# A hybrid decoder step on one core: pooling released from the convolution loop, layer norm's sums inside projection blocks, first output blocks in halves

## The reference

```
h = rmsnorm(x); p = h @ w_in            # columns: conv value | conv gate | pool input, 1024 each
a = v * sigmoid(gate)                   # GLU
y = causal depthwise conv(a), 31 taps   # 8 tiles of 128 channels
yc = silu(layernorm(y + b_dw))          # mean and variance over the 1024 channels
s  = trailing mean of u over 2/4/8/16 positions - u   # 4 groups of 256 channels
yp = (s @ w_pool[group]) * pool_scale
x = x + concat(yc, yp) @ w_out
x = x + hierarchical_moe(rmsnorm(x))    # one group of 4, two of its 8 experts, SwiGLU
return rmsnorm(x), and the last inputs of conv and pooling as new states
```

## Time and profile before

| | us |
|---|---|
| median of 3 executions | 1366.17 |
| lowest and highest | 1365.81, 1368.48 |
| the profiled execution | 1363.6 |
| its span in the trace | 1361.7 |
| TensorE busy in the span | 1257.5 (92%) |
| VectorE, ScalarE, GpSimd busy | 345.9, 115.1, 111.0 |

### The profile page before, as it was taken

The page is one execution under the profiler, slowest core; times in us unless marked ns, Lnnn a source line. Parts: engine busy times, 40 slices in busy tenths (PEclk is TensorE's granted clock), DMA queues, the critical chain, the costliest instruction groups (busy, mean ns, idle before and its releaser), DMA issues.

```text
span 1361.7 us, 16051 instructions
## 1 busy us (share of the span) xinstructions
PE 1257.5 (92%) x6424; PEld 706.8 (52%) x6424; DVE 345.9 (25%) x692; ACT 115.1 (8%) x253; POOL 111.0 (8%) x167
## 2 busy tenths in 40 slices
PE   9999998999999999998989898898989898998894
PEld 7777776777765444454443444444434354444331
DVE  5599963110242110111101011110101011020216
ACT  2100014000210000000000000000000000000003
POOL 3211164000000000000000000000000000000000
PEclk9999999999999999999999999999999999999997
DMA  8544325665459999999999999999999999999985
GB/s 246 167 154 151 124 93 169 215 247 185 152 208 411 424 425 429 427 429 426 429 425 428 427 426 428 425 423 425 424 427 425 429 424 426 417 420 415 388 353 196
DMA packets 82886, 465.13 MB, mean 342 GB/s; under 512 B 7999, under 2 KB 50111, under 8 KB 56691
## 3 DMA queue, kind: packets, MB, share of 16 engines
q1 hardware_dynamic: 77184, 456.41, 82.1%
q0 software_dynamic: 5392, 7.87, 1.9%
q10 hardware_dynamic: 283, 0.48, 0.1%
HBM read 457.20 MB, written 20.80 MB: 351 GB/s over the span
## 4 chain that ended last, share of the span: by engine, by line
DMA 46%; PE 36%; issue 7%; DVE 5%; POOL 3%; SPq 1%; ACT 1%; DVEq 0%; POOLq 0%
DMA arena<-in_w_up_dram 43%; PE bank L759 19%; PE bank L589 11%; DVE arena L1061 3%; PE bank L737 2%; DMA stage<-in_w_down_dram 2%; PE bank L780 2%; POOL arena L1456 1%; DMA arena<-expert_rows 1%; SPq L415 1%; PE bank L674 1%; DMA arena<-in_g_final_dram 1%; POOL arena L1465 0%; PE bank L671 0%; POOL arena L1462 0%
## 5 line engine op out<-in xcount | busy, mean ns | idle before, releaser
L759 PE MATMUL bank<-arena,stage 128*64 128x512 f32 x1920 | 439.4, 611 | 57.0 <-DMA arena<-in_w_up_dram 56.9
L759 PEld LDWEIGHTS bank<-arena,stage 128*64 128x64 f32 x1920 | 145.8, 141 | 343.9 <-issue 304.4
L589 PE MATMUL bank<-arena,stage 128*128 128x288 f32 x1280 | 315.8, 408 | 2.9 <-ACT arena L921 1.5
L589 PEld LDWEIGHTS bank<-arena,stage 128*128 128x128 f32 x1280 | 241.5, 190 | 69.7 <-ACT arena L921 2.0
L737 PEld LDWEIGHTS bank<-x1w,x1r 128*128 128x128 f32 x1536 | 173.9, 192 | 25.2 <-issue 25.2
L737 PE MATMUL bank<-x1w,x1r 128*128 128x128 f32 x1536 | 179.9, 277 | 0.0
L1311 DVE TENSOR_TENSOR a_sb<-sl_sb,bank 128x256 f32<-128x256 f32 x32 | 19.5, 609 | 492.8 <-ACT sl_sb L963 492.8
L780 PE MATMUL bank<-arena,aT 128*64 128x512 f32 x512 | 113.4, 595 | 8.5 <-ACT aT L965 8.5
L1061 DVE SCALAR_TENSOR_TENSOR arena<-arena,wdw 128x256 f32<-128x256 f32 x240 | 102.9, 505 | 0.0
L1473 POOL DMA_INDIRECT expert_rows<-ysb,cur_d x31 | 30.3, 978 | 854.2 <-DVE ysb L1331 827.6
L1331 DVE TENSOR_SCALAR ysb<-bank,wslot 128x512 f32<-128x512 f32 x31 | 23.3, 751 | 254.7 <-PE bank L780 254.7
(11 more groups left out here) (262 smaller groups left out, 483.5 us busy)
## 6 DMA issues: line engine op xcount, KB each, us to landing
arena<-in_w_gate_dram SPq DMA_DIRECT2D x48, 2048.0 KB, 13.9
arena<-in_w_up_dram SPq DMA_DIRECT2D x48, 2048.0 KB, 20.7
arena<-in_w_down_dram SPq DMA_DIRECT2D x30, 2048.0 KB, 17.7
xT<-in_w_down_dram SPq DMA_DIRECT2D x15, 2048.0 KB, 19.8
stage<-in_w_down_dram SPq DMA_DIRECT2D x15, 2048.0 KB, 21.6
arena<-in_w_gate_dram SPq DMA_DIRECT2D x16, 1536.0 KB, 14.8
arena<-in_w_up_dram SPq DMA_DIRECT2D x16, 1536.0 KB, 21.1
stage<-in_w_in_dram SPq DMA_DIRECT2D x11, 2048.0 KB, 8.4
```

Of the source, the lines that this page charges most:

```text
L589: last = pe.matmul(ps[bank][:, 0:NTOK], wsl[a][:, k, cc * P:(cc + 1) * P], rhs[:, k, :], start=(n == 0), stop=(n == KT - 1))
L759: mm = pe.matmul(ps[4 + s][BLK * h:BLK * (h + 1), :], xgT[:, k, BLK * s:BLK * (s + 1)], w[:, :, 256 * h:256 * (h + 1)], start=(k == 0), st ...
```

## The change

There are four edits. The products for new tokens (`prod`) move from `arena` to the tile `ysb`, which is unused until later, GpSimd's loop over the passes is unrolled, and its wait for the end of a pass stands at the head of passes 1 to 3 alone: nothing makes the pooling wait for the fourth pass any more. TensorE's mean product moves into the middle of the sixth pooling-input block, and its variance product ahead of the eighth. The first two w_out blocks are cut in halves, conv channels first, and two of these halves stand between and behind the last w_pool products. ScalarE's list is reordered to suit.

```diff
-        prod = words(arena, O_ST, 2 * NS * W).rearrange("p (c t w) -> p c t w", c=2, t=NS)
+        prod = ysb[:, :, :].rearrange("p s f -> p (s f)")[:, 0:2 * NS * W].rearrange("p (c t w) -> p c t w", c=2, t=NS)
...
-                    dense(2 * c + cc, c, cc, hT).then_inc(u_mm, 1)
-            pool_inputs(0)
-            pool_inputs(1)
-            pool_inputs(2)
-            pe.wait_ge(sum_ready, 1)
-            channel_sum(4, sqw[:, 4:6, :]).then_inc(sum_mm, 1)
-            pool_inputs(3)
-            pe.wait_ge(sq_ready, 1)
-            channel_sum(5, sqw[:, 0:2, :]).then_inc(sumsq_mm, 1)
+                    if m == 3 and cc == 1:
+                        pe.wait_ge(sq_ready, 1)
+                        channel_sum(5, sqw[:, 0:2, :]).then_inc(sumsq_mm, 1)
+                    dense(2 * c + cc, c, cc, hT, between=sum_of_channels if m == 2 and cc == 1 else None).then_inc(u_mm, 1)
+            def sum_of_channels():
+                pe.wait_ge(sum_ready, 1)
+                channel_sum(4, sqw[:, 4:6, :]).then_inc(sum_mm, 1)
+            for m in range(4):
+                pool_inputs(m)
...
+            def out_half(cc, h):
+                for k in range(CT * h, CT * h + CT):
+                    if h == 0 and cc == 0:
+                        pe.wait_ge(mix_ready, k + 1)
+                    last = pe.matmul(ps[cc][:, 0:NTOK], wsl[1][:, k, cc * P:(cc + 1) * P], mixT[:, k, :],
+                                     start=(k == 0), stop=(k == KT - 1))
+                return last
+            for i in range(6):
+                pooled(i)
+            pe.wait_ge(slot_in[1], 16 * 7)
+            out_half(0, 0)
+            pooled(6)
+            pooled(7)
+            out_half(1, 0)
             pe.wait_ge(wp_ready, CT)
-            pooled_first = tuple(range(CT, KT)) + tuple(range(CT))
+            for cc in range(2):
+                out_half(cc, 1).then_inc(o_mm, 1)
...
-            for n in range(6):
+            for n in range(5):
                 pool_line(n)
             act.wait_ge(sum_mm, 1)
             act.activation(nmean[:, :], ps[4][:, 0:NTOK], ACT.Copy, scale=-1.0 / DC).then_inc(nmean_ready, 1)
             act.wait_ge(centred, 1)
             act.activation(words(arena, O_AW, CT * NTOK), words(arena, O_YC, CT * NTOK), ACT.Square).then_inc(squared, 1)
+            pool_line(5)
+            act.activation(preload[:, :], ones[:, 0:1], ACT.Sqrt)
             pool_line(6)
-            pool_line(7)
             act.wait_ge(var_ready, 1)
             act.activation(lnr[:, :], lnv[:, :], ACT.Sqrt).then_inc(sqrt_done, 1)
+            act.activation(silu_table[:, :], ones[:, 0:1], ACT.Silu)
+            pool_line(7)
+            act.wait_ge(yn_ready, 1)
+            for j in range(4):
+                swish(j)
             for i in range(CT):
...
+                pooled(i)
+                if i < 4:
+                    swish(4 + i)
...
-            with pool.Fori(0, 4) as g:
-                ch.loop(g, 1)
+            for g in range(4):
+                if g:
+                    pool.wait_ge(conv_chain, PERC * g)
...
-                pool.wait_ge(conv_chain, PERC * (g + 1))
-            ch.end(4)
+            pool.wait_ge(work_ready, 4)
```

More of the change, by code:

```diff
@@ L652, in _, with pooled @@
             pe.wait_ge(var_ready, 1)
-            for i in range(CT):
+            def pooled(i):
                 g, dd = NG - 1 - i // 2, i % 2
@@ L681, in projection @@
                         pe.wait_ge(slot_in[a], 16 * o + (16 * 7 if a else 16 * 8))
-                    if first and q == 0:
-                        dense(q % 2, a, q % 2, mixT, order=pooled_first, late=(mix_ready, CT)).then_inc(o_mm, 1)
+                    if first and q < 2:
+                        pass
                     elif last and q == 3:
@@ L902, in pool_line, with pooled, swish @@
                          ps[c][:, SEQ:NTOK].rearrange("p (s t) -> p s t", s=NSEQ)).then_inc(u_evac[c // 2], 1)
-            for n in range(6):
+            def pooled(i):
+                act.wait_ge(wp_mm, i + 1)
+                j = CT - 2 - 2 * (i // 2) + i % 2
+                act.activation(mixT[:, CT + j, :], ps[4 + i % 2][:, 0:NTOK], ACT.Copy, scale=pps[:, j:j + 1]).then_inc(wp_ready, 1)
+            def swish(j):
+                act.activation(mixT[:, j, :], yc[:, j, :], ACT.Silu, bias=plb[:, j:j + 1], scale=plg[:, j:j + 1]).then_inc(mix_ready, 1)
+            for n in range(5):
                 pool_line(n)
@@ L909, in _ @@
             act.activation(words(arena, O_AW, CT * NTOK), words(arena, O_YC, CT * NTOK), ACT.Square).then_inc(squared, 1)
+            pool_line(5)
+            act.activation(preload[:, :], ones[:, 0:1], ACT.Sqrt)
             pool_line(6)
-            pool_line(7)
             act.wait_ge(var_ready, 1)
             act.activation(lnr[:, :], lnv[:, :], ACT.Sqrt).then_inc(sqrt_done, 1)
-            for i in range(CT):
[L915 to L921, removed]
+            act.activation(silu_table[:, :], ones[:, 0:1], ACT.Silu)
[3 more added lines that the diff above has]
+                swish(j)
+            for i in range(CT):
+                pooled(i)
+                if i < 4:
+                    swish(4 + i)
             for n, (b, r) in enumerate(((6, AK), (7, AK), (2, UK), (3, UK))):
```

## The result

The changed kernel took 1360.37 us (median of 5, 1358.76 to 1362.09), the kernel before 1368.02 (median of 5, 1365.81 to 1369.84); the ratio is 0.9943, with a 95% interval from 0.9926 to 0.9960, so 5.5 to 10.1 us faster. Forecast was 1371.3, 0.4% slower. Run again later beside other kernels the changed one was at 0.9963 (0.9948 to 0.9977), 3.1 to 7.1 us faster. The two intervals share 5.5 to 7.1 us. The rival "the pass is not held up", with a chance of 0.15, had said 1359.7, a gain of 6.5 us.

What follows compares the result with a forecast made beforehand. The expert-weight stream, started by TensorE, was taken as the bound, carrying mixer changes to the end. Profiled 1363.6 + 9.9 stall + 1.7 low clock - 6.5 tail = 1368.7; with 2.6 for the median, 1371.3 us, range 1362 to 1376.

Steps and rivals of the forecast that it cites:

- the pass is not held up: Fourth convolution pass: GpSimd waits or passes VectorE's taps, no stall, tail's gain alone, 1359.7 us; chance 0.15.
- The bound and the transfer: Mixer to expert weights: the weight stream starts with TensorE, so each mixer microsecond reaches the end one for one.
- the sum: Whole kernel: 1363.6 + 9.9 + 1.7 - 6.5 = 1368.7, plus 2.6 from profiled execution to median, 1371.3 us.
- The tail's gain: Transposes to third w_out block: 27.3 us instead of 33.8, a gain of 6.5 us.
- The new load wait: First half w_out block: its chunk lands 8.1 us after T, wanted at T + 7.7, so 0.4 us wait.
- the halves hide the last group's wait: Mixer tail: the seventh w_pool product comes at T + 11.5, so the 2.71 us wait for pooling goes.
- What the released pooling costs: Fourth convolution pass: 17 pooling instructions take turns with VectorE's taps, and the pass loses 12.9 us.
- The price: Fourth pass: a GpSimd instruction of length p costs the taps p - 0.25, together 12.9 us.
- GpSimd got its second product in against a queue of ready taps: Fourth pass: the argument given against the rival in which the pass is not held up, chance 0.15.
- the stall of 9.9: TensorE in the sixth pooling-input block: waits from 186.4 until `sum_ready` at 196.3, 9.9 us.
- the low clock of 1.7: TensorE's first products behind the stall run at the low clock, costing 1.7 us, 0 to 3 as ends.
- a loss of 9.6 us: Fourth pass: lower end of the forecast's own case, losses 9.6 to 17.1, 1367.5 to 1376 us, chance 0.65.

Runs made afterwards that it cites:

- the twins: Changed kernel with each fourth-pass tap waiting for its immediate predecessor: pooling beside the pass 1377.96 us, pooling held behind it 1372.91 us.
- The memset: Changed kernel with four small GpSimd instructions (a 128-column memset, two copies, an addition) ahead of the pooling: 1358.91 us in one execution.
- the kernels with three gaps: Changed kernel with the fourth pass written out and three of its taps (first of the pair at 14, 18, 22) waiting for their immediate predecessor: 1372.73 us, 1.0045.
- with none: Changed kernel with the fourth convolution pass written out behind a loop of three and no gap in it: 1360.78 us, 0.9937.

## Why the prediction was wrong

- **The bound and the transfer** held as far as the first expert product: it starts 141.6 us behind the third block in both traces. Behind it "one for one to the end" is shown only within the scatter of the weight streaming, 978 to 983 us, and the twins' medians don't show it. The base had moved as well, from 1366.17 (3 executions) to 1368.02 (5), which the sum could not know.
- **The tail's gain** held: 6.5 us predicted, 6.4 in the trace. The new load wait was 0.2 at most, ScalarE's 0.43 instead of 0.1. That the halves hide the last group's wait was a wrong reason: the release and the early order did it before them.
- **"What the released pooling costs"** is the step that failed. It took from L1441 that a GpSimd instruction waiting beside ready taps gets the port after one of them, and so a loss of 12.9 us. Measured loss beside the taps: none, 25.73 us for the pass as before; the addition waited 17 us instead, and TensorE did not stall. The price was not wrong for a case where turns are taken (12.1, 12.9 and 13.0 us measured for 12.9), but the case was. The products at 152.69 and the copy at 154.82 were issued within 0.1 us of GpSimd's last turn; the pooling's first addition comes 5.8 us behind it. "GpSimd got its second product in against a queue of ready taps" is not in the rows either: the product was issued at 152.69, 0.12 us ahead of the first two-input tap at 152.81, and it was the tap that waited. Nothing in the trace of before showed a GpSimd instruction arriving cold in a row of overlapping taps, but the price of the earlier trace rows was carried over as if one had. With no loss the stall of 9.9 and the low clock of 1.7 fall away, and what is left is the tail's 6.5: the first rival.
- **The rule quoted there**, from the Trainium skill's page "SBUF — State Buffer", section "Who interferes with whom", holds in its first half: the memset passed, what reads waited. Its second half, that issue order decides who blocks, does not hold here: some 43 taps issued after the addition, from 162.63 to 179.3, all went ahead of it. The measurement decides.
- **The low clock** was mis-sized: behind a stall of 8.7 us it cost 2.6, behind 15 us (2.29 - 1.13) + (13.69 - 11.80) = 3.1, where I took the 1.7 of a 2.7 us wait and 3 as the end. A smaller slip: a loss of 9.6 us gives 1368.0 by the prediction's own sum, not 1367.5.
- **The rival's own argument** ("VectorE's taps follow so closely that GpSimd gets its turns only in gaps") was right for an instruction that comes late, and its counter-evidence was what misled me. It is not the whole of it, since GpSimd gets turns without a gap too while its last read is recent. All the turns behind the 12.9 were of one kind, GpSimd just busy; for that a chance of 0.15 was low, and the range left the case out.

## What to carry to other kernels

A contended resource has two possible losers, and a trace shows only who lost in the state it was in: ask how the waiting instruction arrived, not only that the two collided. Releasing GpSimd work beside a dense row of two-input VectorE instructions may be harmless to the row (it is simply shut out, and meets what comes behind the row: here `sum_ready` 2 us later) or cost three quarters of its own length, and a semaphore wait that opens 0.04 us gaps, or a tiny GpSimd instruction shortly before, can turn one into the other: here 12 us between the medians of the kernels with three gaps and with none. When a change has several parts, test them one by one: here the release alone or the new orders alone gave most of the gain, ScalarE's order needed the early sums, and the halves gave nothing.

## What the runs showed of the hardware

- Overlapping VectorE instructions with two SBUF inputs (issued every 0.40 us, 0.47 to 0.48 long) kept a GpSimd read out for 17 us, until they ended; a gap of 0.04 us let it in. Writing alone was not kept out (one memset, 0.21 us). The section on the chip says that the engines meet only at semaphores; by these rows VectorE and GpSimd also meet where they read SBUF.
- GpSimd was let in between the same overlapping instructions when it had been idle for up to 2.81 us behind an instruction that read, and was not from 4.53 us on. I had expected no memory of this kind. What sets that time, and where the memory sits, stays open; all these rows are from the fourth pass, with one kind of VectorE instruction, and no run varied its length.
- In turns, 17 GpSimd instructions of 17.1 us cost the taps 12.1 to 13.0 us, and nine of 9.5 us cost them 7.3.
- TensorE's granted clock behind a stall, in the run with three gaps (columns: stretch, its length, busy us of PE, PEld, DVE, ACT and POOL, granted clock, DMA share, GB/s):

```profile
189.00:195.00 6.00, 0.00 (x0) 0.00 (x0) 5.83 (x10) 0.00 (x0) 0.00 (x0) 0.58 0.00 0
195.30:200.00 4.70, 4.70 (x10) 3.42 (x11) 1.98 (x1) 0.41 (x1) 0.00 (x0) 0.50 0.00 0
201.00:203.00 2.00, 2.00 (x10) 1.58 (x9) 0.23 (x1) 1.88 (x2) 0.00 (x0) 1.00 0.04 8
```

It fell to 0.50, the 1.2 GHz level, while TensorE waited, and was back at 1.00 when it had worked for about 5 us, against under 4 behind the wait of 2.71 us.
